# Weight splits earlier by GpSimd, the high part of x first, and spare matmuls moved in a two-layer network on one core

## The chip, the cores and the metric

The kernel runs on one core of a Trainium2 chip (trn2). The metric is the device time of one execution in microseconds (us), all of the network from its inputs in HBM to its output there. The kernel before takes 2657.98 us, the median of 3 runs (2656.43 to 2665.24).

The engines are named as the profile names them: PE (TensorE matmuls), PEld (its weight loads), DVE (VectorE), ACT (ScalarE), POOL (GpSimd), SP (SyncE, which here only issues the loads of weights).

## What is computed

Three layers on 512 tokens of width 1024, in float32, from the reference:

```python
# layer 0: h += norm(gmlp(norm(h)));  h += norm(sq_relu_mlp(norm(h)))            hidden 4096
# layer 1: k, v = norm(h) @ w_k, w_v; h += norm(band attention(norm(h), k, v)); h += norm(sq_relu_mlp(norm(h)))
def gmlp_spatial_gating(h, w_in, ln_g, ln_b, w_s, b_s, w_out):
    u, v = split(gelu(h @ w_in));  v = layer_norm(v);  return (u * (w_s masked @ v + b_s)) @ w_out
# block 2
h = h + 0.5 * swiglu(rms_norm(h), w_gate, w_up, w_down)                          # hidden 2816
z = rms_norm(h) @ w_in   # aq ak av iq ik iw | rq rk rv rg | ga gb
score = sum_heads(relu(iq . ik) * iw);  top 128 keys of each query;  y_a = softmax attention on these
y_r = group_norm(retention(rq, rk, rv)) * silu(rg)
h = h + (sigmoid(ga) * (y_a @ w_a) + sigmoid(gb) * (y_r @ w_b)) @ w_out
h = h + 0.5 * swiglu(...);  h = h + sigmoid(rms_norm(h) @ w_ple_gate) * (p @ w_ple_proj);  return rms_norm(h)
```

## The kernel before, in words

**Layout.** Activations lie feature-major: 8 tiles of 128 features by 512 tokens. The residual stream is `H`. A normed input is never divided by its root mean square before the product: `x = H * gain` goes into the product, and the result is scaled by `RI` (1 / rms, spread over all partitions) when it is taken out of PSUM.

**Three passes.** Every product runs in fp32r with both operands split into a high and a low part, as `WH*XH + WH*XL + WL*XH` (`three_passes`, L418): three matmuls of 128x128 by 128x512 for each of 8 tiles of the contraction.

**Units.** The weights are 411 units of 128x1024, in one order for all engines (`PRODUCTS`, L61): gmlp_v 0, gmlp_u 8, gmlp_out 16, ffn_a0 24, att_v 88, att_kq 96, att_out 112, ffn_a1 120, ffn_b1 184, mix_heads 252, ret_qk 263, ret_v 271, ret_gate 279, merge 287, mix_out 319, ffn_b2 327, ple 395. For each, SP loads `RAW[u % 4]` as soon as unit u-4 is split, and one engine pair splits it: POOL does both parts in the ranges of `POOL_RANGES` (high L362, low L365), elsewhere ACT makes the high part (`split_high`, L865) and DVE the low one (`split_low`, L1205), eight units (`AHEAD`) ahead of the unit whose result they take. The parts lie in slots: 0 to 3 are `WH`/`WL`, 4 to 7 (only inside the ranges of `WIDE`) are `WH2`/`WL2` or another free place (`weights_of`, L301). A unit is split only when the unit that had its slot is done (`slot_before`, L107).

**Synchronisation.** There is no scheduler: each engine's program is written out in order, and waits are on semaphores that count units done, evacuated, split. `split_low(u)` of the first unit behind a POOL range waits until POOL has split all of the range (L1209 and L1210); so does `split_high` for the high parts.

**Between two products.** The sum of squares `SS` needs all 8 result tiles: ACT squares (`square`, L875), DVE adds (`add_square`, L1217). PE turns it into a column (`stat`, L504), ACT takes the root, DVE the reciprocal (`recip`, L1237), PE spreads it (`spread`, L513). Then `post_and_pre` (L1257) forms the new `H` tile by tile and `pre_tile` (L1229) adds the square and writes `XL`, while ACT (`pre_norm`, L882) squares and then writes `XH`. The first group of the next product goes through all its units tile by tile (`together`, L436, or for token-major results `token_major_half`, L470), each tile as soon as its `XL` is there (semaphore `x_ready`); its own stat comes before the last tile (`before_last`). After a gated ffn this is `half_step` (L1362), which needs no stat of the branch.

**Attention.** The band attention runs in 32 pair steps, between which PE works on q, k and att_out tiles. In the mixing block, `mix_heads` gives the index queries and keys, each rotated by DVE and ACT (`rotate`, L1529); PE then needs the transposed `T` (L770) and `index_ready`. The sparse attention is two rounds (`attention_round`, L553, L970 and L1376) of 16 score tiles each, in 19 steps; step n has scores of n (L565), transposes of n-2 (L575), values of n-3 (L586), and `keep_busy` (L548, L551) issues matmuls that write a bank nobody reads.

## Time and profile before

| | |
|---|---|
| Runs | 2657.98 us median of 3 (2656.43 to 2665.24) |
| Profiled execution, its own time | 2656.32 us |
| its span, first to last instruction | 2654.5 us |
| PE busy | 2468.9 us (93%) in 11064 matmuls |
| DVE busy | 1363.6 us (51%) |
| ACT busy | 760.3 us (29%) |
| POOL busy | 609.3 us (23%) |
| mean granted TensorE clock | 0.968 of full |
| read from HBM | 218.23 MB, 83 GB/s over the span |

A busy share is a mean over the whole span. The 1.8 us between span and time lie around the span. Stretches are given as times from the span's start. Matmuls are pipelined: a 128x512 matmul is recorded with 0.39 us, and the next one starts 0.226 us after it (0.43 us at the halved clock).

### The profile page before, as it was taken

The numbers are of one execution on the slowest core, as the hardware profiler recorded it, in microseconds if no ns is written. First come the engines' busy times: TensorE is split into PE (matmuls) and PEld (weight loads), VectorE is DVE, ScalarE is ACT, GpSimd is POOL, SyncE is SP. The second block draws the span as 40 slices with busy tenths as digits, with TensorE's granted clock in tenths as the row PEclk, the third lists the DMA queues.
The fourth block names the chain that finished last, engine by engine and source line by source line (L and its number), as shares of the span: only waits on it lengthen the run. The fifth ranks groups of instructions, "written<-read, shape, count | busy, mean of one in ns | idle before, by whom it ended". The sixth has DMA issues, their size and how long they took to land.

```text
span 2654.5 us, 29957 instructions
## 1 busy us (share of the span) xinstructions
PE 2468.9 (93%) x11064; PEld 1972.6 (74%) x11064; DVE 1363.6 (51%) x1947; ACT 760.3 (29%) x1200; POOL 609.3 (23%) x283
## 2 busy tenths in 40 slices
PE   6778999989996999998999997979989997999997
PEld 5667888877665788887888886556578885888886
DVE  4546434463663643445554356797444353544464
ACT  2114323331442422333322233312322111322232
POOL 7650000024435000000000005462037875000000
PEclk9898999999998999999999998989999998999999
DMA  4222333322222233332433331121012332333321
GB/s 168 74 84 65 111 97 101 94 65 71 84 65 87 64 105 100 96 91 64 119 96 96 90 93 56 48 72 40 16 40 84 98 95 85 105 104 93 91 81 54
DMA packets 64824, 221.81 MB, mean 84 GB/s; under 512 B 7504, under 2 KB 9680, under 8 KB 64592
## 3 DMA queue, kind: packets, MB, share of 16 engines
q1 hardware_dynamic: 59184, 208.17, 26.5%
q10 hardware_dynamic: 5536, 12.19, 1.4%
q8 instruction: 73, 1.20, 0.2%
q14 instruction: 31, 0.25, 0.0%
HBM read 218.23 MB, written 2.10 MB: 83 GB/s over the span
## 4 chain that ended last, share of the span: by engine, by line
PE 81%; DVE 10%; POOL 4%; ACT 3%; issue 2%; ACTq 0%; POOLq 0%; DVEq 0%
PE PS L420 23%; PE PS L422 22%; PE PS L421 22%; PE PS L489 3%; POOL WH L362 2%; POOL WL L365 2%; PE PS L551 1%; DVE WL L1214 1%; PE PS L780 1%; PE PS L696 1%; PE PS L565 1%; PE PS L717 1%; PE PS L586 1%; PE PS L706 1%; DVE MK L1582 1%
## 5 line engine op out<-in xcount | busy, mean ns | idle before, releaser
L420 PE MATMUL PS<-XH,WH 128*128 128x512 f32 x1792 | 713.1, 398 | 40.3 <-DVE T L1433 12.5
L421 PE MATMUL PS<-XL,WH 128*128 128x512 f32 x1792 | 701.7, 392 | 0.0
L422 PE MATMUL PS<-XH,WL 128*128 128x512 f32 x1784 | 699.1, 392 | 0.0
L362 POOL TENSOR_TENSOR WH<-RAW,ONES 128x1024 fp32r<-128x1024 f32 (+1 forms) x136 | 266.1, 1957 | 1623.9 <-PE PS L422 1502.1
L1214 DVE TENSOR_TENSOR WL<-RAW,WH 128x1024 fp32r<-128x1024 f32 (+2 forms) x272 | 322.5, 1186 | 248.3 <-ACT WH L873 192.1
L420 PEld LDWEIGHTS PS<-XH,WH 128*128 128x128 f32 x1792 | 339.2, 189 | 130.3 <-issue 33.8
L420 PE MATMUL PS<-HH,WH 128*128 128x512 f32 x992 | 389.1, 392 | 2.5 <-DVE HL L1286 2.5
L422 PEld LDWEIGHTS PS<-XH,WL 128*128 128x128 f32 x1784 | 337.7, 189 | 71.9
L421 PEld LDWEIGHTS PS<-XL,WH 128*128 128x128 f32 x1792 | 339.8, 190 | 67.6
L422 PE MATMUL PS<-HH,WL 128*128 128x512 f32 x992 | 386.2, 389 | 0.0
L421 PE MATMUL PS<-HL,WH 128*128 128x512 f32 x992 | 386.1, 389 | 0.0
L873 ACT ACTIVATE WH<-RAW 128x1024 fp32r<-128x1024 f32 (+2 forms) x272 | 276.7, 1017 | 349.6 <-DVE M L1317 202.5
L365 POOL TENSOR_TENSOR WL<-RAW,WH 128x1024 fp32r<-128x1024 f32 (+1 forms) x132 | 322.4, 2442 | 10.4
L420 PEld LDWEIGHTS PS<-HH,WH 128*128 128x128 f32 x992 | 186.2, 188 | 50.0 <-issue 9.1
L422 PEld LDWEIGHTS PS<-HH,WL 128*128 128x128 f32 x992 | 186.2, 188 | 39.0
L421 PEld LDWEIGHTS PS<-HL,WH 128*128 128x128 f32 x992 | 186.3, 188 | 37.7
L1286 DVE TENSOR_TENSOR HL<-T,HH 128x512 fp32r<-128x512 f32 x108 | 74.8, 692 | 127.1 <-ACT HH L936 92.7
L489 PE MATMUL PS<-WH,XH 128*128 128x512 f32 x192 | 80.9, 421 | 47.2 <-DVE XL L1234 21.9
L1226 DVE TENSOR_TENSOR SS<-SS,T 128x512 f32<-128x512 f32 x91 | 82.9, 910 | 24.6 <-ACT T L879 24.6
L933 ACT ACTIVATE T<-T 128x512 f32<-128x512 f32 x64 | 40.5, 632 | 185.0 <-DVE T L1293 185.0
L1317 DVE TENSOR_TENSOR M<-PS,M 128x512 f32<-128x512 f32 x48 | 33.2, 691 | 107.2 <-PE PS L422 106.8
L879 ACT ACTIVATE T<-H 128x512 f32<-128x512 f32 x72 | 45.4, 631 | 140.3 <-DVE H L1263 47.8
(210 smaller groups left out, 2452.6 us busy)
## 6 DMA issues: line engine op xcount, KB each, us to landing
RAW<-in_weights SPq DMA_DIRECT2D x379, 512.0 KB, 3.5
RAW<-in_weights SPq DMA_DIRECT2D x16, 384.0 KB, 3.2
H<-in_xT ACTq DMA_DIRECT2D x8, 256.0 KB, 9.1
BIAS<-in_rel ACTq DMA_DIRECT2D x8, 256.0 KB, 3.6
RAW<-in_weights SPq DMA_DIRECT2D x8, 256.0 KB, 2.7
out<-R ACTq DMA_DIRECT2D x8, 256.0 KB, 2.2
BIAS<-in_rel ACTq DMA_DIRECT2D x8, 224.0 KB, 3.9
DECAY<-in_decay ACTq DMA_DIRECT2D x1, 1024.0 KB, 4.7
```

Of the source, the lines that this page charges most:

```text
L362: nc.gpsimd.tensor_tensor(high[:, 0:w], raw, ONES[:, 0:1].to_broadcast([P, w]), ALU.mult).then_inc(high_split, 1)
L365: nc.gpsimd.tensor_tensor(low[:, 0:w], raw, high[:, 0:w].bitcast(F32), ALU.subtract).then_inc(weights_split, 1)
L420: nc.tensor.matmul(PS[:, bank_, :], high[:, w], xh[:, k, :], start=(k == 0), stop=False)
L421: nc.tensor.matmul(PS[:, bank_, :], high[:, w], xl[:, k, :], start=False, stop=False)
L422: return nc.tensor.matmul(PS[:, bank_, :], low[:, w], xh[:, k, :], start=False, stop=stop)
L489: last = nc.tensor.matmul(PS[:, (first + j) % SLOTS, :], x[:, k, tok], wt[:, w], start=(k == 0 and n == 0), stop=(k == DT - 1 and n == 2))
L873: S.activation(weights_of(u)[0][:, 0:w], RAW[:, slot, 0:w], ACT.Copy).then_inc(high_split, 1)
L879: S.activation(T[:, sq.n % 2, :], src, ACT.Square).then_inc(sq_ready, 1)
L933: S.activation(T[:, 1, :], T[:, 0, :], ACT.Square).then_inc(act_self, 1)
L1214: V.tensor_tensor(low[:, 0:w], RAW[:, slot, 0:w], high[:, 0:w].bitcast(F32), ALU.subtract).then_inc(weights_split, 1)
L1226: V.tensor_tensor(SS[:], SS[:], T[:, slot, :], ALU.add).then_inc(ss_ready, 1)
L1286: V.tensor_tensor(HL[:, f, :], T[:, src, :], HH[:, f, :].bitcast(F32), ALU.subtract).then_inc(h_ready, 1)
```

## The change

- **Slots.** `WIDE` begins 4 units earlier before ffn_a0 (20 in place of 24), before ffn_a1 (116 for 120) and 8 earlier before ffn_b2 (323 for 331). Units 20 to 23 are split into `WLA`/`WL2` and wait for no unit; 116 to 119 into `WHB`/`WLB` (where `XH` and `XL` lay), from the end of unit 111 on; 323 to 326 into `WHX`/`WL2`, from the end of the merge (unit 318) on. 24 to 27 and 120 to 123 get slots 0 to 3, behind 16 to 19 and 112 to 115. Since the slots alternate by fours, the other end of each wide range shifts too: 88 to 91 now lie in slots 0 to 3, so 92 to 95 wait for them (before, for 84 to 87); 252 to 255 lie in slots 4 to 7, so 256 to 259 wait for 248 to 251 (before, for 252 to 255). POOL's last range ends at 331, and units 331 to 334 are split by ACT and DVE.
- **High part first.** ACT writes `XH` of a tile before it squares it. DVE writes `XL` (`low_part`) before it forms the next `H` and before it adds the square. In the first groups of gmlp_v, ffn_a0, att_v, ffn_a1, ffn_b1, mix_heads and ffn_b2, PE waits for `XH` alone (`xh_ready`), does both passes with it, and only then waits for `XL`.
- **Spare matmuls.** `keep_busy(24, 7)` is added before the wait ahead of L770; in the sparse attention the 2 spare matmuls of each of 18 steps are gone in both rounds, while the 10 before each round and the 14 in step 1 stay.

The core of the diff:

```diff
-POOL_RANGES = ((0, 28), (92, 124), (256, 335))
+POOL_RANGES = ((0, 28), (92, 124), (256, 331))
 AHEAD = 8
 
-WIDE = ((24, 92, 20), (120, 256, 116), (331, UNITS, 328))
+WIDE = ((20, 92, 16), (116, 256, 112), (323, UNITS, 319))
...
-            high = WHA[:, k - SLOTS, :] if 331 < u < 335 else WH2[:, k - SLOTS, :]
-            low = WLA[:, k - SLOTS, :] if 120 <= u < 124 else WL2[:, k - SLOTS, :]
+            high = WHX[k - SLOTS] if 323 <= u < 335 else WLA[:, k - SLOTS, :] if u < 24 else \
+                WHB[:, k - SLOTS, :] if 116 <= u < 120 else WH2[:, k - SLOTS, :]
+            low = WLB[:, k - SLOTS, :] if 116 <= u < 120 else WLX[k - SLOTS] if 124 <= u < 128 else WL2[:, k - SLOTS, :]
...
                     pool.wait_ge(landed[v % SLOTS], 16 * (v // SLOTS + 1) + step * 16)
-                    if v == 24:
-                        pool.wait_ge(x_ready, 2 * DT)
-                    elif v == 120:
-                        pool.wait_ge(x_done, 2 * DT * TT)
-                    elif v == 332:
+                    if v == FIRST["att_out"] + SLOTS:
+                        pool.wait_ge(units_done, FIRST["att_out"] + SLOTS)
+                    elif v == FIRST["mix_out"] + SLOTS:
                         pool.wait_ge(units_done, FIRST["mix_out"] + SLOTS)
                     elif slot_before(v) is not None:
                         pool.wait_ge(units_done, slot_before(v) + 1 + SLOTS + step * SLOTS)
...
                 for k in range(deepest):
                     if k == deepest - 1 and before_last:
                         before_last()
+                    if high:
+                        pe.wait_ge(xh_ready, high(k))
+                        w = slice(k * P, k * P + P)
+                        for s, (tiles, xh, xl, ready) in enumerate(units):
+                            if k == 0:
+                                pe.wait_ge(weights_split, split.next())
+                                pe.wait_ge(evacuated, bank.next())
+                            for n, part in enumerate(weights_of(first + s)):
+                                nc.tensor.matmul(PS[:, (first + s) % SLOTS, :], part[:, w], xh[:, k, :],
+                                                 start=(k == 0 and n == 0), stop=False)
+                        pe.wait_ge(ready.sem, ready.now(back=tiles - 1 - k))
+                        for s, (tiles, xh, xl, ready) in enumerate(units):
+                            last = nc.tensor.matmul(PS[:, (first + s) % SLOTS, :], weights_of(first + s)[0][:, w],
+                                                    xl[:, k, :], start=False, stop=(k == tiles - 1))
+                            if k == tiles - 1:
+                                last.then_inc(units_done, 1)
+                        continue
                     for s, (tiles, xh, xl, ready) in enumerate(units):
                         kk = k - (deepest - tiles)
...
                         k = 2 * q + kk
                         if k == DT - 1 and before_last:
                             before_last()
-                        if ready is not None:
-                            pe.wait_ge(ready.sem, ready.now(back=DT - 1 - k))
                         w = slice(kk * SEQ, kk * SEQ + SEQ)
-                        for j in range(TT):
-                            tok = slice(j * P, j * P + P)
-                            for n, (x, wt) in enumerate(((XH, high), (XL, high), (XH, low))):
-                                last = nc.tensor.matmul(PS[:, (first + j) % SLOTS, :], x[:, k, tok],
-                                                        wt[:, w], start=(k == 0 and n == 0),
-                                                        stop=(k == DT - 1 and n == 2))
+                        if high_now:
+                            pe.wait_ge(xh_ready, high_now(k))
+                        for passes in ((XH, high), (XH, low)), ((XL, high),):
+                            if ready is not None and passes[0][0] is XL:
+                                pe.wait_ge(ready.sem, ready.now(back=DT - 1 - k))
+                            for j in range(TT):
+                                tok = slice(j * P, j * P + P)
+                                for x, wt in passes:
+                                    last = nc.tensor.matmul(PS[:, (first + j) % SLOTS, :], x[:, k, tok], wt[:, w],
+                                                            start=(k == 0 and x is XH and wt is high),
+                                                            stop=(k == DT - 1 and x is XL))
...
                     if n < 16:
                         scores(n)
                     if not ahead:
-                        keep_busy(14 if n == 1 else 2, 2)
...
             xr.next(DT)
-            together(*[(DT, XH, XL, xr)] * 3, before_last=stat)
+            xp.n = 7 * DT
+            together(*[(DT, XH, XL, xr)] * 3, before_last=stat, high=lambda k: xp.now() + k + 1)
             spread(5)
             for s in range(3):
                 product(DT, XH, XL)
             v_ready = bank.now() + SLOTS
             product(DT, XH, XL)
+            keep_busy(24, 7)
             pe.wait_ge(evacuated, v_ready)
             for j in range(TT):
...
             def pre_norm(gs, free, ready, evacuates=None):
 
 
+                act.wait_ge(units_done, free + SLOTS)
                 for t in range(DT):
                     act.wait_ge(ready.sem, ready.next())
-                    square(H[:, t, :])
-                    if t == 0:
-                        act.wait_ge(units_done, free + SLOTS)
-                    for g, dst in gs:
+                    for n, (g, dst) in enumerate(gs):
                         S.activation(dst[:, t, :], H[:, t, :], ACT.Copy, scale=gain(g, t)).then_inc(xh_ready, 1)
+                        if n == 0:
+                            square(H[:, t, :])
                     if evacuates is not None:
                         split_high(evacuates + t + AHEAD)
...
+            def low_part(t, g, dh, dl, ready):
+
+                dve.wait_ge(xh_ready, xh.next())
+                V.scalar_tensor_tensor(dl[:, t, :], H[:, t, :], gain(g, t), dh[:, t, :].bitcast(F32),
+                                       ALU.mult, ALU.subtract).then_inc(ready, 1)
+
+            def square_and_rest(t, gs):
+
+                add_square(t == 0)
+                for g in gs[1:]:
+                    low_part(t, *g)
+
             def pre_tile(t, gs):
 
-                add_square(t == 0)
-                for g, dh, dl, ready in gs:
-                    dve.wait_ge(xh_ready, xh.next())
-                    V.scalar_tensor_tensor(dl[:, t, :], H[:, t, :], gain(g, t), dh[:, t, :].bitcast(F32),
-                                           ALU.mult, ALU.subtract).then_inc(ready, 1)
+                low_part(t, *gs[0])
+                square_and_rest(t, gs)
...
                 for t in range(DT + 1):
                     if t < DT:
                         z = T[:, 2 + t % 2, :]
-                        link(V.tensor_tensor(z, m[:, t, :], PS[:, 4, :], ALU.mult))
+                        V.tensor_tensor(z, m[:, t, :], PS[:, 4, :], ALU.mult).then_inc(dve_self, 1)
+                        me.next()
+                    if t:
+                        low_part(t - 1, *gs[0])
+                    if t < DT:
+                        dve.wait_ge(dve_self, me.now())
                         V.scalar_tensor_tensor(H[:, t, :], z, gain(g_out, t), H[:, t, :],
                                                ALU.mult, ALU.add).then_inc(residual, 1)
                     if t:
-                        pre_tile(t - 1, gs)
+                        square_and_rest(t - 1, gs)
...
                         z = T[:, 2 + t % 2, :]
                         V.tensor_tensor(z, src, M[:, t, :], ALU.add).then_inc(evacuated, 1)
+                    if t:
+                        low_part(t - 1, *gs[0])
+                    if t < DT:
                         dve.wait_ge(evacuated, done.now())
                         V.scalar_tensor_tensor(H[:, t, :], z, 0.5, H[:, t, :], ALU.mult, ALU.add)\
                          .then_inc(residual, 1)
                     if t:
-                        pre_tile(t - 1, gs)
+                        square_and_rest(t - 1, gs)
                         split_low(u + t - 1 + AHEAD)
```

**Where instructions move, 1.** POOL from unit 18 to unit 21 (one loop turn of units 4 to 19, its last two units, then the block that follows the loop), before:

```order
L361 REGISTER_ALU [waits weights_landed2]
L362 TENSOR_TENSOR WH_72<-RAW_71,ONES_107 128x1024 [waits units_done]
L365 TENSOR_TENSOR WL_73<-RAW_71,WH_72 128x1024 [waits weights_high_split]
L361 REGISTER_ALU [waits weights_landed3]
L362 TENSOR_TENSOR WH_72<-RAW_71,ONES_107 128x1024 [waits units_done]
L365 TENSOR_TENSOR WL_73<-RAW_71,WH_72 128x1024 [waits weights_high_split]
L380 REGISTER_ALU
L380 COMPARE_AND_BRANCH
L362 TENSOR_TENSOR WH2_74<-RAW_71,ONES_107 128x1024 [waits x_parts_ready,weights_landed0]
L365 TENSOR_TENSOR WL2_75<-RAW_71,WH2_74 128x1024 [waits weights_high_split]
L362 TENSOR_TENSOR WH2_74<-RAW_71,ONES_107 128x1024 [waits weights_landed1]
L365 TENSOR_TENSOR WL2_75<-RAW_71,WH2_74 128x1024 [waits weights_high_split]
```

and now, from the block that follows the loop through the first of the units behind it:

```order
L382 REGISTER_ALU
L382 COMPARE_AND_BRANCH
L364 TENSOR_TENSOR WLA_76<-RAW_71,ONES_116 128x1024 [waits weights_landed0]
L367 TENSOR_TENSOR WL2_75<-RAW_71,WLA_76 128x1024 [waits weights_high_split]
L364 TENSOR_TENSOR WLA_76<-RAW_71,ONES_116 128x1024 [waits weights_landed1]
L367 TENSOR_TENSOR WL2_75<-RAW_71,WLA_76 128x1024 [waits weights_high_split]
...
L364 TENSOR_TENSOR WLA_76<-RAW_71,ONES_116 128x1024 [waits weights_landed3]
L367 TENSOR_TENSOR WL2_75<-RAW_71,WLA_76 128x1024 [waits weights_high_split]
L364 TENSOR_TENSOR WH_72<-RAW_71,ONES_116 128x1024 [waits units_done,weights_landed0]
L367 TENSOR_TENSOR WL_73<-RAW_71,WH_72 128x1024 [waits weights_high_split]
```

Before, the block behind the loop is units 24 to 27 and begins with a wait for the end of the reads of `x` (`x_parts_ready`), behind units 20 to 23, which waited in the loop for `units_done`. Now it is units 20 to 23 and waits for no `units_done`, only for the landed weights; 24 and on stand behind it.

**Where instructions move, 2.** DVE in the norm ahead of att_v, tiles 1 and 2 (`T<-M,PS` and `H` are `post_and_pre`, `XL` and `HL` the low parts for the two products, `SS` the sum of squares), before:

```order
L1262 TENSOR_TENSOR T_92<-M_50,PS 128x512
L1263 SCALAR_TENSOR_TENSOR H_49<-T_92,GAIN_108,H_49 128x512 [waits dve_self]
L1226 TENSOR_TENSOR SS_93<-SS_93,T_92 128x512 [waits squares_ready,square_sum_ready]
L1234 SCALAR_TENSOR_TENSOR XL_54<-H_49,GAIN_108,XH_53 128x512 [waits high_ready]
L1234 SCALAR_TENSOR_TENSOR HL_57<-H_49,GAIN_108,HH_56 128x512 [waits high_ready]
```

and now:

```order
L1297 TENSOR_TENSOR T_101<-M_50,PS 128x512
L1258 SCALAR_TENSOR_TENSOR XL_54<-H_49,GAIN_117,XH_53 128x512 [waits high_ready]
L1303 SCALAR_TENSOR_TENSOR H_49<-T_101,GAIN_117,H_49 128x512 [waits dve_self]
L1252 TENSOR_TENSOR SS_102<-SS_102,T_101 128x512 [waits squares_ready,square_sum_ready]
L1258 SCALAR_TENSOR_TENSOR HL_57<-H_49,GAIN_117,HH_56 128x512 [waits high_ready]
```

`XL` of a tile now stands ahead of the next `H` and of the add of the square; the number of operations is the same.

**Where instructions move, 3.** PE in steps 2 and 3 of a round of the sparse attention (L565 and now L584 scores, L551 and now L570 spare matmuls, L575 and now L594 transposes, L586 and now L605 values), before:

```order
L565 MATMUL PS<-AK_63,T_92 128x384 [waits scores_read]
L551 MATMUL PS<-XH_53 128x512 x2
L575 MATMUL PS<-IDENT_106,PB_95 128x128 [waits probs_ready]
...
L565 MATMUL PS<-AK_63,T_92 128x512 [waits scores_read]
L551 MATMUL PS<-XH_53 128x512 x2
L575 MATMUL PS<-IDENT_106,PB_95 128x128 [waits probs_ready]
L575 MATMUL PS<-IDENT_106,PB_95 128x128
L584 REGISTER_ALU [waits probs_t_ready]
L586 MATMUL PS<-PTB_96,AVW_65 64x128 [waits hidden_parts_ready]
```

and now:

```order
L584 MATMUL PS<-AK_63,T_101 128x384 [waits scores_read]
L594 MATMUL PS<-IDENT_115,PB_104 128x128 [waits probs_ready]
...
L584 MATMUL PS<-AK_63,T_101 128x512 [waits scores_read]
L594 MATMUL PS<-IDENT_115,PB_104 128x128 [waits probs_ready]
L594 MATMUL PS<-IDENT_115,PB_104 128x128
L603 REGISTER_ALU [waits probs_t_ready]
L605 MATMUL PS<-PTB_105,AVW_65 64x128 [waits hidden_parts_ready]
```

Between scores and transposes nothing is left; all waits stay.

## Rows read from the trace of the kernel before

**Rows 1.** the page: shares of the chain of work that ended last, by engine

```profile
PE 81%; DVE 10%; POOL 4%; ACT 3%; issue 2%; ACTq 0%; POOLq 0%; DVEq 0%
```

**Rows 2.** waits of PE: engine, line <- releaser: us in total, times, longest us

```profile
PE PS L509 <- DVE SS L1226: 45.1, 5, 19.0
...
PE PS L770 <- DVE T L1547: 14.0, 1, 14.0
...
PE PS L420 <- POOL WL L365: 9.8, 4, 4.1
PE PS L420 <- DVE T L1305: 9.1, 1, 9.1
```

**Rows 3.** timeline, POOL and DVE, the gates of layer 0: start us, us, engine, line, operation [idle before]

```profile
133.64 2.35 POOL L365 TENSOR_TENSOR WL<-RAW,WH 128x1024 fp32r<-128x1024 f32 x1
...
133.80 2.73 DVE L1443 TENSOR_TENSOR T<-T,R 128x512 f32<-128x512 f32 x1
...
137.37 0.69 DVE L1443 TENSOR_TENSOR T<-T,R 128x512 f32<-128x512 f32 x1
```

**Rows 4.** timeline, PE and ACT, the end of gmlp_out and the start of ffn_a0

```profile
204.08 1.86 PE L509 MATMUL PS<-ONES,SS 128*128 128x1 f32 x8 [18.12 <-DVE SS L1226]
...
210.20 0.63 ACT L879 ACTIVATE T<-H 128x512 f32<-128x512 f32 x1 [3.96 <-DVE H L1263]
...
212.70 0.77 PE L420 MATMUL PS<-XH,WH 128*128 128x512 f32 x1 [4.11 <-DVE XL L1234]
```

**Rows 5.** timeline, DVE, the norm ahead of att_v, two tiles in a row

```profile
592.89 0.74 DVE L1234 SCALAR_TENSOR_TENSOR XL<-H,GAIN,XH 128x512 fp32r<-128x512 f32 x1
...
596.20 0.74 DVE L1234 SCALAR_TENSOR_TENSOR XL<-H,GAIN,XH 128x512 fp32r<-128x512 f32 x1
```

**Rows 6.** timeline, DVE, the last pair steps of the band attention

```profile
786.27 2.55 DVE L1513 TENSOR_SCALAR PROB<-PROB,RECX 128x512 f32<-128x512 f32 x1
```

**Rows 7.** timeline, POOL and DVE, the end of att_out

```profile
833.10 1.90 POOL L362 TENSOR_TENSOR WH<-RAW,ONES 128x1024 fp32r<-128x1024 f32 x1
...
850.36 1.22 DVE L1214 TENSOR_TENSOR WL<-RAW,WH 128x1024 fp32r<-128x1024 f32 x1 [21.44 <-POOL WLA L365]
```

**Rows 8.** timeline, DVE, the rotations of mix_heads

```profile
1622.65 0.68 DVE L1531 TENSOR_TENSOR T<-PS,RI 128x512 f32<-128x512 f32 x1
...
1630.05 0.68 DVE L1531 TENSOR_TENSOR T<-PS,RI 128x512 f32<-128x512 f32 x1
...
1652.75 0.69 DVE L1531 TENSOR_TENSOR T<-PS,RI 128x512 f32<-128x512 f32 x1
...
1657.44 0.28 DVE L1560 TENSOR_SCALAR SC<-RELU,AVW 128x128 f32<-128x128 f32 x1
```

**Rows 9.** the chain of waits in order of time (start us, us, what), sparse attention

```profile
1838.18 1.05 PE PS L565 x2
1839.24 0.66 PE PS L551 x2
...
1847.65 0.62 PE PS L565
```

**Rows 10.** groups of DVE by line, 1826 to 1910 us: xcount | busy us, mean ns | idle before

```profile
L1601 DVE TENSOR_TENSOR PB<-PS,MK 128x256 f32<-128x256 f32 (+3 forms) x31 | 15.4, 496 | 26.4 <-PE PS L565 26.3
L1389 DVE TENSOR_REDUCE NM<-PB 128x1 f32<-128x256 f32 (+3 forms) x31 | 15.3, 493 | 1.1
...
L1396 DVE TENSOR_SCALAR PB<-PB,REC 128x128 f32<-128x128 f32 (+3 forms) x32 | 12.4, 387 | 1.1
...
L1395 DVE RECIPROCAL REC<-SUM 128x1 f32<-128x1 f32 x32 | 4.9, 154 | 0.7 <-ACT PB L980 0.7
```

**Rows 11.** timeline, PE, the first product of ffn_b2

```profile
2206.81 0.80 PE L420 MATMUL PS<-XH,WH 128*128 128x512 f32 x1 [3.40 <-POOL WL L365]
```

**Rows 12.** windows: us, PE PEld DVE ACT POOL busy, PE clock, DMA share, GB/s

```profile
1640.40:1657.50 17.10, 6.85 (x17) 4.23 (x17) 12.41 (x14) 6.26 (x12) 7.09 (x3) 0.50 0.21 65
1819.50:1910.00 90.50, 89.88 (x417) 54.95 (x418) 52.60 (x144) 37.75 (x105) 0.00 (x0) 1.00 0.02 6
```

37 lines of the change are left out of this document (23 added, 14 removed).

## The prediction

> **What bounds the kernel now.** The page first: the chain of work that ended last is PE for 81% of the span, DVE for 10% and POOL for 4% [rows 1]. So only what PE waits for can be won. The table of PE's waits names it next [rows 2]: 45.1 us in five waits for the last sum of squares, the longest 19.0; 14.0 us ahead of the transposes at L770; 9.8 us for low weight parts that POOL makes, all at the start of ffn_b2; 9.1 us for DVE one product later. The timelines then tell what is late behind each name. Last come the windows, for the clock [rows 12]: in the stretch after the 14 us wait PE is granted 0.50 of full speed (1.2 GHz) for 17.1 us, in the sparse attention 1.00. A wait of PE therefore costs twice: itself, and work that runs at half pace behind it.
>
> The second thing to price is how POOL and DVE get in each other's way, since the change moves 20 unit splits of POOL forward, beside DVE's work. In the gates of layer 0 a DVE multiply of two SBUF operands takes 2.73 us when POOL's low part (2.35 us) has just begun, and 0.69 us three microseconds later [rows 3]: 2.04 us lost. A unit has two POOL operations, so up to 4.1 us of DVE per unit. In the rotations one head takes 7.40 us beside POOL (1622.65 to 1630.05) and 4.69 us without (1652.75 to 1657.44) [rows 8], 2.7 us lost in 7.4, or 1.8 us per 4.9 us of splitting. The gates are the nearer row where DVE works back to back; a DVE operation may come in the middle of POOL's, so I take 3.4 us per unit there. By the Trainium skill (GPSIMD Engine Reference, Specifications) the SBUF interfaces of GpSimd are shared with VectorE, with contention for DVE instructions that have two SBUF inputs. It speaks against splitting earlier. By the rule the trace agrees, 2.73 against 0.69 us. An account without that rule would price all moved splits at nothing: rival A.
>
> **The terms.** All against the profiled execution's own 2656.3 us. Parts with one answer go together.
>
> 1. *Start, gmlp_v.* `XH` ahead of the square lets PE begin its two high passes earlier, but the tiles come in by DMA, and only the order of ACT's two operations changes. POOL's operations fall elsewhere among DVE's. +1.5 (-3 to +4).
>
> 2. *gmlp_out (units 20 to 23 early).* The wait for the sum at its end is 18.12 us [rows 4], since DVE may split unit 28 on only when POOL has finished 24 to 27, and then squares. POOL is through one block of four earlier. Without contention the wait shrinks to about 2.6 (the last tile's evacuation, square and add, 0.6 to 0.7 each as such operations take [rows 3, 4], and handoffs): -15.6. But 20 to 23 are now split while the gates run: 8 two-input operations of DVE lose 2.04 each, 16.3. PE starts the product late and is paced by `XL`. Some lies in slack; I take 11.6: **-4.0** (bounds -15.6 and +0.7).
>
> 3. *High first at ffn_a0, ffn_a1, ffn_b1.* PE waits 4.11 us for the first `XL` [rows 4]. `XH` came behind the square of 0.63 us and was followed by DVE's next `T`, `H`, the copy and `XL`. `XH` can now be made where the square was, from 210.20 on, and stands at 210.9; the high passes start then instead of at 212.70 and cover DVE's low part: -1.7 each, **-5.1** (-7 to -2). The square is later by one ACT operation, 0.7, which the 8 tiles' DVE cadence hides.
>
> 4. *att_v.* DVE sets the pace, five operations and 3.31 us per tile (592.89 to 596.20) [rows 5]. Units 92 to 95 used to wait for 84 to 87; now for 88 to 91, so 92 to 94 are split beside these very operations, four in five of which have two SBUF inputs. 3 units x 3.4 = 10.2, less 3.5 of slack that PE leaves and high first, plus 1.2 of slow clock: **+7.6** (-1 to +12).
>
> 5. *Pair steps (116 to 119 early).* They are now split back to back from the end of unit 111. A DVE scale of one pair step already takes 2.55 us beside POOL [rows 6], and there its steps are near PE's pace. Four units x 3.4 = 13.6 bounds it, half and more is slack: **+4.0** (0 to +8).
>
> 6. *att_out.* This is the clearest one. DVE's low part at 850.36 stood 21.44 us, released by POOL's `WLA`, since POOL began unit 120 only at 833.10 [rows 7]: four units of 4.8 us behind the reads of the attention output. Now 116 to 119 are done before, 120 to 123 take the place of 116 to 119, and DVE comes free 17 us earlier, about 833. Late next is the last square itself: the 19.0 us wait [rows 2] becomes 2.6: **-16.4** (-19 to -10).
>
> 7. *mix_heads.* 256 to 259 start four units of PE earlier (4 x 24 x 0.226 = 22 us), since they wait for 248 to 251 and not for 252 to 255. They slow the half step ahead (+2), then leave two or three of the rotations free of POOL, 2.7 us each. L770 starts some 3.6 us earlier. `keep_busy(24, 7)` takes 24 x 0.23 = 5.4 us at full clock (about 10 at half), which ends inside a wait of 10 or more; the gain in clock is about 1.5. Sum **-5.0** (-9 to 0). If the wait were shorter than the spare matmuls, they would cost what reaches over.
>
> 8. *Sparse attention.* Two spare matmuls are 0.66 us in each step [rows 9], 18 steps, two rounds: 23.8 at most. In four steps PE spends 9.47 (1838.18 to 1847.65) [rows 9], without the spare ones 6.83. What comes next is the ring of two steps: scores of n-1, DVE's add and maximum, the scaling of n-2, its transposes, values of n-3, scores of n+1. By means: PE 9.47/4 less 0.66 = 1.71 of scores, transposes and values; DVE 0.496 + 0.493 + 0.154 + 0.387 = 1.53 [rows 10]; handoffs, five of about 0.1, an estimate. That is 3.7 to 3.8 for two steps, 7.6 for four, and as the long steps of PE and DVE do not coincide, near 8.2. (9.47 - 8.2) x 4.5 = 5.9 a round: **-11.8** (0 to -23.8, where the ring does or does not bind throughout).
>
> 9. *ffn_b2 (323 to 326 early, 331 to 334 by ACT and DVE).* POOL's last unit is 330, and it begins as soon as the merge ends. The 9.8 us for low parts go [rows 2]. The group at 2206.81 [rows 11] then starts when DVE gives `XL` tiles, still 2.5 us behind where the waits summed would put it; the 9.1 us for `T` [rows 2], which DVE made late as it had waited for POOL, go; 2.2 of slow clock behind these waits goes. -9.8 - 9.1 - 2.2 + 2.5 = **-18.6** (-23 to -14).
>
> Sum: +1.5 - 4.0 - 5.1 + 7.6 + 4.0 - 16.4 - 5.0 - 11.8 - 18.6 = -47.8, so 2608.5, told as **2609**. The median of the runs is 1.7 above the profiled execution, less than the sum is sure of.
>
> **The rivals.**
>
> *A, contention is light, or the ring is slack.* For it: POOL is busy 23% of the span only, and a DVE operation that comes between POOL's is not held. Against: rows 3 show 2.04 us at once. Then term 2 is -15.6, term 4 -1, term 5 nothing: -24 more, **2584**. The full 23.8 of term 8 alone would give 2597.
>
> *B, contention is heavy.* Each of the 20 moved units costs PE its whole 3.4 us: 68 instead of the 23 counted in terms 2, 4 and 5: 45 more, **2654**, no change. For it: DVE is the pace in att_v. Against: most moved splits lie beside products of PE that have DVE idle (it is busy 51%).
>
> *C, the clock falls in the sparse attention.* It ends slower. Its steps stay at 1.00 now [rows 12] with spare matmuls of full width in each; without them PE has short matmuls and transposes, 6.83 of 8.2 us. At 1.2 GHz its own work in four steps is 13.7 us, over the ring, and each round 13.7 x 4.5 + 3.9 of head = 65.5 against 46.2 now: +38.6 for two in place of -11.8, and some 5 for the retention head behind at half clock: **2664**, slower than before by 0.3%; each us that att_v or the gates lose above my terms goes on top. Below a granted clock of 0.72 the steps' own work (6.83/0.72 = 9.5) gives back term 8; to end slower than before it needs the lower clock through both rounds. Against it: PE stays over 80% busy. The Trainium skill (TensorE: Matmul & The Clock Gate, Part 4: PE-mode transpose) says that full clock does not engage for transposes, which do not count as busy the same way. No run here shows this by itself so far.
>
> *D, the change does less than it says:* the ring holds steps at 9.4 us already, term 8 is nothing, **2620**.
>
> **The numbers.** Forecast 0.60 (D is in its range), A 0.17, B 0.14, C 0.09. A measurement of this kernel can tell about 0.3%, 8 us, from no change. The bounds of the unknown terms, added as independent, give some 20 about the forecast; the range takes in A to 2587 and most of B, to 2648, and leaves out C and the low end of A. Faster by over 0.3% is the forecast, A, and B's better part, 0.60 + 0.17 + 0.09 = 0.86; within 0.3%, the rest of B and half of C, 0.09; slower 0.05.
>
> **What would show it.** Right: the wait for the sum ahead of ffn_a1 is 2 to 4 us; no wait of PE for POOL's low part ahead of ffn_b2, whose first tile starts near 6 us after where it did; rows at 0.77 and 2.7 us side by side on DVE in the gates; four sparse steps in 8.2 us at clock 1.00. Wrong: att_out's wait still over 10 us (then DVE is held by something else); sparse steps at 9.4 or 6.9 us per four; a PE clock under 1.00 there; a wait for POOL in att_v ahead of unit 96.

## The result, and the profile after

The changed kernel takes 2638.28 us (median of 4 runs, 2633.09 to 2638.75) where the kernel before, run beside it, takes 2660.94 (2656.43 to 2665.24). The ratio is 0.9911, 95% interval 0.9887 to 0.9934: faster by 0.9%, 22.7 us between the medians, about half of the 47.8 that were forecast. The profiled execution has a span of 2636.9 us (before 2654.5) and a mean clock of 0.961 (before 0.968). It is the slowest of its four runs, and the one before is the fastest, so the stages below differ by 17.6 us in all.

Stage by stage in the two profiled executions, each stage from the first instruction named to the next one's:

| Stage | before, us | after, us | difference | forecast |
|---|---|---|---|---|
| start to the wait ahead of the gates | 95.6 | 97.1 | +1.5 | +1.5 |
| to the first tile of ffn_a0 | 117.1 | 109.2 | -7.9 | -5.7 |
| ffn_a0, to the sum ahead of att_v | 357.2 | 356.9 | -0.3 | 0 |
| att_v, to the first tile of its second product | 64.2 | 75.0 | +10.8 | +7.6 |
| pair steps and att_out, to the sum | 226.5 | 212.6 | -14.0 | -12.4 |
| ffn_a1 and ffn_b1, to the sum in mix_heads | 750.2 | 748.1 | -2.1 | -3.4 |
| mix_heads, to the transposes of the index inputs | 39.8 | 33.8 | -6.0 | -5.0 |
| to the first retention tile (index scores, sparse attention) | 264.7 | 283.4 | **+18.7** | **-11.8** |
| to the first tile of ffn_b2, and from there to the end | 739.1 | 720.8 | -18.3 | -18.6 |

All rows but one came within 3.2 us of the forecast. The chain of work that ended last, by engine, in the changed kernel (before [rows 1]):

```profile
PE 80%; DVE 12%; ACT 3%; issue 2%; POOL 2%; ACTq 0%; POOLq 0%; DVEq 0%
```

POOL went from 4% of the chain to 2%, DVE from 10 to 12. The waits of PE in the changed kernel (engine, line <- releaser: us in total, times, longest):

```profile
PE PS L528 <- DVE SS L1252: 19.6, 7, 4.6
...
PE PS L422 <- DVE T L1476: 12.5, 1, 12.5
...
PE PS L453 <- ACT XH L915: 7.4, 3, 2.5
PE PS L508 <- POOL WL L367: 7.2, 2, 3.6
...
PE PS L594 <- DVE PB L1439: 4.2, 7, 0.9
...
PE PS L453 <- DVE H L1707: 3.5, 2, 2.3
...
PE PS L795 <- DVE T L1590: 2.4, 1, 2.4
```

Against [rows 2]: the sums fell from 45.1 us to 19.6, the longest from 19.0 to 4.6; the index inputs' 14.0 are 2.4; POOL's 9.8 at ffn_b2 (L420, now L453) are gone, and 3.5 for `H` stand there instead; the 9.1 are gone too. The 12.5 us ahead of the gates are as they were. Nothing in this table tells of a loss of 19 us in the sparse attention: it isn't a wait. The windows show it (us, then busy time of PE, PEld, DVE, ACT, POOL, then PE clock, DMA share, GB/s), the whole of the two rounds in the changed kernel:

```profile
1801.00:1821.90 20.90, 18.91 (x84) 11.50 (x83) 17.18 (x45) 8.90 (x24) 1.20 (x1) 1.00 0.09 26
1821.90:1852.60 30.70, 29.84 (x89) 16.96 (x90) 12.58 (x35) 9.69 (x30) 0.00 (x0) 0.50 0.00 1
1852.60:1866.30 13.70, 12.15 (x55) 7.70 (x53) 6.31 (x19) 6.18 (x15) 0.00 (x0) 1.00 0.00 1
1866.30:1910.70 44.40, 43.47 (x129) 24.85 (x130) 17.85 (x48) 13.04 (x39) 0.00 (x0) 0.50 0.00 0
```

PE is granted 1.00 for the first 20.9 us, then 0.50 (1.2 GHz) for 30.7, 1.00 for 13.7 and 0.50 for 44.4. Before, both rounds had 1.00 [rows 12]. The timeline of PE, the scores of steps four apart, at either clock:

```profile
1812.33 0.49 PE L584 MATMUL PS<-AK,T 64*128 64x128 f32 x2
...
1820.44 0.48 PE L584 MATMUL PS<-AK,T 64*128 64x128 f32 x2
...
1827.27 1.65 PE L584 MATMUL PS<-AK,T 64*128 64x384 f32 x2
...
1840.80 1.01 PE L584 MATMUL PS<-AK,T 64*128 64x384 f32 x1
```

Four steps take 8.11 us at full clock (1812.33 to 1820.44; 8.2 was forecast, 9.47 before [rows 9]) and 13.53 at half (1827.27 to 1840.80). The 13.7 us at 1.00 in the middle are not plain steps: they lie around the end of the first round and hold the 10 and 14 full-width spare matmuls of the second round's head (from 1853.83 and 1857.81 on).

### The profile page after: what moved, and what is told of

It is laid out like the page before. It is cut to its first block, busy times and chain, and to the rows that moved or that the text cites. A ratio compares the mean times of both kernels' runs of the same rounds, so it can differ in the third digit from the quotient of the medians.

```text
span 2636.9 us, 29784 instructions
## 1 busy us (share of the span) xinstructions
PE 2494.5 (95%) x11016; PEld 1986.7 (75%) x11016; DVE 1397.0 (53%) x1951; ACT 764.5 (29%) x1204; POOL 594.9 (23%) x275
## 4 chain that ended last, share of the span: by engine, by line
PE 80%; DVE 12%; ACT 3%; issue 2%; POOL 2%; ACTq 0%; POOLq 0%; DVEq 0%
PE PS L422 22%; PE PS L424 21%; PE PS L423 21%; PE PS L453 2%; PE PS L508 2%; PE PS L457 1%; PE PS L605 1%; DVE MK L1625 1%; PE PS L584 1%; DVE SS L1252 1%; DVE TOP L1624 1%; POOL WL L367 1%; PE PS L805 1%; PE PS L717 1%; PE PS L738 1%
## 5 line engine op out<-in xcount | busy, mean ns | idle before, releaser
L422 PE MATMUL PS<-XH,WH 128*128 128x512 f32 x1600 | 634.7, 397 | 18.1 <-DVE T L1476 12.5
L424 PE MATMUL PS<-XH,WL 128*128 128x512 f32 x1632 | 638.1, 391 | 0.0
L423 PE MATMUL PS<-XL,WH 128*128 128x512 f32 x1600 | 625.2, 391 | 0.0
L364 POOL TENSOR_TENSOR WH<-RAW,ONES 128x1024 fp32r<-128x1024 f32 (+1 forms) x123 | 239.9, 1950 | 1589.8 <-DVE WL L1240 735.9
L422 PEld LDWEIGHTS PS<-XH,WH 128*128 128x128 f32 x1600 | 302.0, 189 | 98.3 <-issue 20.9
L424 PEld LDWEIGHTS PS<-XH,WL 128*128 128x128 f32 x1632 | 307.8, 189 | 65.2
L423 PEld LDWEIGHTS PS<-XL,WH 128*128 128x128 f32 x1600 | 302.4, 189 | 60.2
L367 POOL TENSOR_TENSOR WL<-RAW,WH 128x1024 fp32r<-128x1024 f32 (+1 forms) x123 | 300.5, 2443 | 9.6
L1252 DVE TENSOR_TENSOR SS<-SS,T 128x512 f32<-128x512 f32 x91 | 91.7, 1008 | 24.6 <-ACT T L905 24.6
L508 PE MATMUL PS<-WL,XH 128*128 128x512 f32 x192 | 81.6, 425 | 0.0
```

Of the source, the lines that this page charges most:

```text
L364: nc.gpsimd.tensor_tensor(high[:, 0:w], raw, ONES[:, 0:1].to_broadcast([P, w]), ALU.mult).then_inc(high_split, 1)
L367: nc.gpsimd.tensor_tensor(low[:, 0:w], raw, high[:, 0:w].bitcast(F32), ALU.subtract).then_inc(weights_split, 1)
L422: nc.tensor.matmul(PS[:, bank_, :], high[:, w], xh[:, k, :], start=(k == 0), stop=False)
L423: nc.tensor.matmul(PS[:, bank_, :], high[:, w], xl[:, k, :], start=False, stop=False)
L424: return nc.tensor.matmul(PS[:, bank_, :], low[:, w], xh[:, k, :], start=False, stop=stop)
L508: last = nc.tensor.matmul(PS[:, (first + j) % SLOTS, :], x[:, k, tok], wt[:, w], start=(k == 0 and x is XH and wt is high), stop=(k == DT ...
```

## Experiments

Theory: all terms hold but the one of the sparse attention, whose spare matmuls were what kept the clock. Rival: contention of POOL and DVE ate the gain. Each run is compared with the kernel before on the same chip, so across experiments the ratios are safer to compare than the times. Lines in the rows are those of the version that ran; where its edit adds lines, they lie a few further down than in the changed kernel. Stages and rows come from one profiled execution each.

### 1. The spare matmuls back

```diff
-                        keep_busy(14 if n == 1 else 0, 2)
+                        keep_busy(14 if n == 1 else 2, 2)
```

> The changed kernel with the 2 spare matmuls back in each step of the sparse attention; all else as changed. Theory (clock): the sparse attention alone lost the rest, because PE falls to 1.2 GHz in it. Then the granted clock of both rounds is 1.00 again, four steps take 9.47 us as before the change, the stretch is some 18 us shorter than in the changed kernel, and the time is 2618 to 2622 us, ratio to before 0.984 to 0.986. Rival (contention): the early splits of POOL lost it, the sparse stretch moves by under 5 us and the time stays at 2633 to 2640.

2619.45 us (2614.43 to 2626.42), ratio 0.9856 (0.9833 to 0.9878). The two rounds in the windows of this version:

```profile
1798.00:1842.50 44.50, 44.33 (x209) 27.25 (x210) 26.74 (x73) 17.17 (x51) 0.00 (x0) 1.00 0.01 4
1842.50:1887.00 44.50, 43.80 (x207) 26.57 (x205) 23.88 (x66) 18.18 (x52) 0.00 (x0) 1.00 0.00 0
```

Clock 1.00 throughout. The stretch from the transposes of the index inputs to the first retention tile is 262.8 us, within 2 us of what it was before the change, and the median is 18.8 us below that of the changed kernel (by the two ratios, 0.9911 and 0.9856, it is 14.6; the intervals don't touch). The theory holds, the rival doesn't.

### 2. Only this part, in the kernel before

```diff
-                        keep_busy(14 if n == 1 else 2, 2)
+                        keep_busy(14 if n == 1 else 0, 2)
```

> The kernel before with one part of the change: no spare matmuls in the steps of the sparse attention. Theory (clock): this part by itself costs; the clock falls to 0.50 within the first round, four steps go from 9.47 to 13.5 us there, and the time is before + 15 to 20, ratio 1.006 to 1.008. Rival (the fall needs another part of the change, such as the earlier start or the 24 spare matmuls ahead): clock 1.00, four steps in 8.1 us, ratio 0.995 to 0.996. Third case: as the clock falls at a time that lies differently to the steps, the loss may be anywhere from 5 to 39 us.

2678.01 us (2664.50 to 2679.96), ratio 1.0067 (1.0050 to 1.0084): slower, 19 us by the medians. The windows of the rounds:

```profile
1819.00:1850.10 31.10, 27.81 (x128) 16.31 (x126) 24.25 (x67) 14.37 (x41) 0.80 (x1) 1.00 0.06 18
1850.10:1867.20 17.10, 16.30 (x54) 10.29 (x54) 5.44 (x15) 4.29 (x13) 0.00 (x0) 0.50 0.00 1
1867.20:1887.60 20.40, 18.34 (x82) 10.86 (x81) 12.07 (x35) 10.08 (x27) 0.00 (x0) 1.00 0.00 0
1887.60:1918.30 30.70, 29.84 (x91) 17.29 (x91) 11.99 (x32) 9.02 (x27) 0.00 (x0) 0.50 0.00 0
```

The same fall, without any other part of the change. Counted from the first spare matmul ahead of the rounds (1815.17, in the changed kernel 1797.58) it begins 35 us in, not 24, and 47.8 us of the rounds are at 0.50 in place of 75.1; this profiled execution (2664.5) is the mildest of its five. When the fall begins varies; it came in both executions that were profiled, and the other four times are longer still.

### 3. One spare matmul per step

```diff
-                        keep_busy(14 if n == 1 else 0, 2)
+                        keep_busy(14 if n == 1 else 1, 2)
```

> The changed kernel with 1 spare matmul in each step in place of 0. PE's own work in four steps is then 6.83 + 4 x 0.33/1.45 = about 7.7 to 8.15 us, the ring of DVE and PE gives about 8.2 to 8.6. Theory (clock, held by what PE does in the steps): if one spare matmul holds the clock, four steps take about 8.6 us, the time is 8 us below the version with two, 2610 to 2614, ratio 0.981 to 0.983. If it does not hold it, the steps take about 15 us at half clock, and the time is that of the changed kernel or more, 2636 to 2655. Rival (contention): within 5 us of the changed kernel's 2638 either way.

2616.21 us (2613.31 to 2622.03), ratio 0.9840 (0.9818 to 0.9861). Both rounds at clock 1.00:

```profile
1797.00:1842.00 45.00, 43.76 (x200) 26.48 (x198) 31.66 (x82) 18.59 (x52) 2.98 (x2) 1.00 0.05 15
1842.00:1887.00 45.00, 43.15 (x203) 25.85 (x202) 24.15 (x66) 19.18 (x53) 0.00 (x0) 1.00 0.00 0
```

One holds the clock as two do. Four steps take 9.0 us, not the expected 8.6: PE waits once in four steps, behind the 512-wide scores, and runs back to back in the other three, so a spare matmul in those costs its whole time, 0.3 us (9.01 us against 8.11 for three of them). From the start of ret_v to the first retention tile it is 4.5 us less than with two (146.5 against 151.0).

### 4. The spare matmuls only where PE waits

```diff
-                        keep_busy(14 if n == 1 else 0, 2)
+                        keep_busy(14 if n == 1 else 4 if n % 4 == 0 else 0, 2)
```

> The changed kernel with 4 spare matmuls in every fourth step (the one whose transposes wait for DVE's scaling behind the 512-wide scores) and none in the others: as many in four steps as with one per step, but all where PE waits, 1.28 us in each four steps. Theory (the clock needs enough matmul work per stretch, no matter in which step): clock 1.00 in both rounds, four steps in 8.1 to 8.3 us in place of 9.0, so 7 to 8 us below the version with one spare per step: 2608 to 2610. Rival (the three steps without any pull the clock down): clock 0.50 in part of the rounds as in the changed kernel, four steps up to 14 to 15 us, 2632 to 2640.

2611.04 us (2609.69 to 2618.37), ratio 0.9826 (0.9808 to 0.9844).

```profile
1796.00:1840.00 44.00, 43.28 (x208) 27.11 (x207) 31.37 (x82) 18.71 (x52) 2.80 (x2) 1.00 0.05 16
1840.00:1884.00 44.00, 42.70 (x199) 26.21 (x198) 24.06 (x66) 19.29 (x53) 0.00 (x0) 0.96 0.00 0
```

The clock holds but for a moment (0.96 in the second round), and from the start of ret_v to the first retention tile it is 1.7 us less than with one per step. Less than expected: four steps take 8.4 us, and step 0 got 4 spare matmuls where it had 1, which costs 0.7 in each round.

### 5. Units 20 to 23 as before

```diff
-WIDE = ((20, 92, 16), (116, 256, 112), (323, UNITS, 319))
+WIDE = ((24, 92, 20), (116, 256, 112), (323, UNITS, 319))
```

with two spare matmuls per step, and POOL's wait for the reads of `x` ahead of unit 24 as before the change.

> The changed kernel with 2 spare matmuls per step and with units 20 to 27 and so the slots up to unit 91 as before the change (20 to 23 wait in slots 0 to 3, 24 to 27 wide; 92 to 95 wait for 84 to 87 again). Theory (terms by stage hold): gmlp_out and its sum's wait lose the gain of 6 us, att_v gains 12.8 us back as POOL no longer splits 92 to 95 beside the norm's DVE operations (3.3 us a tile as before instead of longer). So 6 us faster than the version with the two spare matmuls alone: 2612 to 2616. Rival (POOL and DVE do not hurt each other in att_v, the loss there is from the new order of low part and square): att_v stays 12 us longer, and the time is 2624 to 2628.

2619.57 us (2618.74 to 2626.54), ratio 0.9846 (0.9830 to 0.9863): as experiment 1, no gain. By stages both parts are there: ffn_a0's first tile comes 7.2 us later behind the gates' wait (the sum's wait is 18.1 again, as in [rows 4]), and att_v takes 68.5 us in place of the 74.6 of experiment 1. It was expected to fall back to 64. DVE's tiles take 3.2 us there; the rest is 13.6 us at 0.50 behind the sum where before the change it was 3.4. The profiled execution is the longest of the four and loses 5.2 us more ahead of the gates, where the edit changes nothing. Inconclusive for the time, since the terms cancel; experiment 6 tells it.

### 6. Units 16 to 19 early in their place

```diff
-WIDE = ((20, 92, 16), (116, 256, 112), (323, UNITS, 319))
+WIDE = ((16, 92, 12), (116, 256, 112), (323, UNITS, 319))
...
-            high = WHX[k - SLOTS] if 323 <= u < 335 else WLA[:, k - SLOTS, :] if u < 24 else \
+            high = WHX[k - SLOTS] if 323 <= u < 335 else WLA[:, k - SLOTS, :] if u < 20 else \
```

with POOL's waits ahead of unit 24, and one spare matmul per step. Then the alternation by fours comes out as before the change: 92 to 95 lie in slots 0 to 3 and wait for 84 to 87.

> The changed kernel with 1 spare matmul per step, and in place of units 20 to 23 now units 16 to 19 lie in the early place and wait for no unit; 20 to 23 wait in slots 0 to 3 for 12 to 15, 24 to 27 lie wide and wait for 20 only, so that 92 to 95 wait for 84 to 87 as before the change. Theory (contention in att_v costs about 6 us there, the early split in gmlp_out brings 6): both are had, the stat ahead of ffn_a0 stays at a wait of 2.2 us, att_v's tiles on DVE take 3.2 us, and the time is 5 to 8 us below the version with one spare matmul (2616): 2608 to 2611, ratio 0.981 to 0.983. Rival (the gates' contention moves to an earlier product and the gain of gmlp_out goes with it): 2614 to 2620.

2607.41 us (2601.01 to 2608.16), ratio 0.9806 (0.9790 to 0.9823), 8.8 us below the version with one spare. att_v takes 64.1 us; in the version with one spare it was 77.7. (Some of that is chance: six profiled executions with the same att_v code, those of the changed kernel and of experiments 1, 3, 4, 8 and 12, took 74.6 to 77.7.) What POOL does to DVE there is seen in the changed kernel, timelines of POOL and DVE:

```profile
583.01 2.35 POOL L364 TENSOR_TENSOR WH<-RAW,ONES 128x1024 fp32r<-128x1024 f32 x1 [1.88 <-PE PS L508]
585.44 2.69 POOL L367 TENSOR_TENSOR WL<-RAW,WH 128x1024 fp32r<-128x1024 f32 x1
594.17 1.97 POOL L364 TENSOR_TENSOR WH<-RAW,ONES 128x1024 fp32r<-128x1024 f32 x1 [6.04 <-PE PS L508]
596.23 2.68 POOL L367 TENSOR_TENSOR WL<-RAW,WH 128x1024 fp32r<-128x1024 f32 x1
```

```profile
583.52 0.68 DVE L1297 TENSOR_TENSOR T<-M,PS 128x512 f32<-128x512 f32 x1
584.12 1.78 DVE L1258 SCALAR_TENSOR_TENSOR XL<-H,GAIN,XH 128x512 fp32r<-128x512 f32 x1
585.83 2.85 DVE L1303 SCALAR_TENSOR_TENSOR H<-T,GAIN,H 128x512 f32<-128x512 f32 x1
...
594.32 2.38 DVE L1303 SCALAR_TENSOR_TENSOR H<-T,GAIN,H 128x512 f32<-128x512 f32 x1
596.62 2.83 DVE L1252 TENSOR_TENSOR SS<-SS,T 128x512 f32<-128x512 f32 x1
```

and of PE, at the end of the same tiles:

```profile
601.43 0.80 PE L528 MATMUL PS<-ONES,SS 128*128 128x1 f32 x3 [4.62 <-DVE SS L1252]
```

Two DVE operations that start 0.39 us after POOL's low part take 2.85 and 2.83 us where they otherwise take 0.74 and 0.68, and those beside POOL's high parts 1.78 and 2.38 where they otherwise take 0.74. All four end 0.54 to 0.56 us after the POOL operation they started beside, and so do the two beside the unit before (576.49 and 579.40, 2.38 and 2.28 us long). `T`, which reads one of its inputs from PSUM, took 0.68 in the middle of one (583.52). For the three units that is 3.2, 3.2 and 3.8 us of DVE, 10.1 together, and PE waits 4.62 us for the sum. In experiment 6 every tile takes 3.19 us (585.06 to 588.25 for two low parts in a row):

```profile
585.06 0.75 DVE L1261 SCALAR_TENSOR_TENSOR XL<-H,GAIN,XH 128x512 fp32r<-128x512 f32 x1
...
588.25 0.75 DVE L1261 SCALAR_TENSOR_TENSOR XL<-H,GAIN,XH 128x512 fp32r<-128x512 f32 x1
```

The rival had a point too. Earlier splits cost elsewhere: the wait ahead of the gates is 19.7 us instead of 12.5, and the sum ahead of ffn_a0 waits 6.84, not 2.2:

```profile
199.47 1.87 PE L531 MATMUL PS<-ONES,SS 128*128 128x1 f32 x8 [6.84 <-DVE SS L1255]
```

### 7. att_v low first

```diff
-            products_token_major(xr, stat, lambda k: xp.now() + 2 * k + 1)
+            products_token_major(xr, stat)
```

PE then waits for the low part ahead of all three passes there. One spare matmul per step.

> The version with 1 spare per step, but PE in the first half of att_v waits for the low part of each tile before all three passes, as before the change; DVE's order stays new. Theory (high first there lets PE catch up with DVE, which sets the pace, so that it stands at the sum and its clock falls): no or a short wait at the stat, att_v from its first stat to the second half's start 3 to 5 us shorter, 2611 to 2613. Rival (contention with POOL alone makes att_v longer): same as the version with one spare, 2615 to 2618.

2614.22 us (2611.54 to 2616.96), ratio 0.9834 (0.9818 to 0.9851), against 2616.21 with high first; the intervals overlap. att_v takes 77.8 us against 77.7. The forecast 3 to 5 us don't show: high first there costs nothing that these runs can tell, though one profile of each, where the same code varies by 3 us, wouldn't show less.

### 8. Without the 24 ahead of the transposes

```diff
-            keep_busy(24, 7)
```

with one spare matmul per step.

> The version with 1 spare per step, without the 24 spare matmuls ahead of the transposes of the index inputs. Theory (they lie in a wait and only keep the clock): the wait ahead of the transposes is 8 to 10 us long, they start at the same moment, and some 1.5 to 3 us are lost at half clock behind it: 2617 to 2620. Rival (the clock gate needs them not, or they delay the transposes): 0 to 2 us faster, 2614 to 2616.

The ten runs gave 2614.76 once, 2649.78 to 2661.29 nine times, median 2658.37. Neither expectation has it. The windows, from 1631.1 us on, the index scores:

```profile
1631.10:1733.50 102.40, 97.21 (x170) 45.15 (x171) 39.68 (x55) 26.44 (x52) 19.06 (x9) 0.50 0.07 21
```

The clock fell 5.2 us ahead of the transposes (1636.29), inside a wait of 7.81, and stayed: PE is busy for 97.2 of 102.4 us, all of it at 0.50. This is work of three full-width matmuls to one narrow score. In the changed kernel the same work is at 1.00 but for 6.8 us.

### 9. The 24 alone, in the kernel before

```diff
             product(DT, XH, XL)
+            keep_busy(24, 7)
             pe.wait_ge(evacuated, v_ready)
```

> The kernel before with one part of the change alone: the 24 spare matmuls ahead of the transposes of the index inputs. Theory (they shorten the idle time from 14 to about 8 us and so the stretch at 0.50 behind it from 17 to 7 to 14 us): 1.5 to 5 us faster than before, ratio 0.998 to 0.9995; the transposes start at the same moment. Rival (as in the version without them, the wait of 8 us that they leave may be followed by 100 us at 0.50): 2680 to 2700, ratio 1.01 or more, or very different single runs.

2658.89 us (2656.39 to 2697.21, 10 runs), ratio 0.9996 (0.9986 to 1.0006, without the run of 2697.21). The half-clock stretch goes from 17.1 us to 6.8 in the profile, but most of the 17.1 lies inside the wait: PE works 6.85 us of it, and 3.5 of the 6.8. The time doesn't move beyond its uncertainty. One run of ten took 2697.21, and one of seven of the kernel before in another comparison 2698.91; neither was profiled.

### 10. Low first in all first groups

Experiment 6 with `high=` and `high_now` left out of all calls, so that PE waits for the low part ahead of the three passes everywhere.

> The version with units 16 to 19 early and 1 spare per step, but PE waits for the low part of each tile before all three passes in all first groups, as before the change; the orders of ACT and DVE stay new. Theory (high first starts each of four groups 1.7 us earlier, but at half clock, so 1.0 to 1.3 us each are left): 4 to 6 us slower than with high first, 2611 to 2614, the waits ahead of these groups 3.1 to 3.4 us in place of 2.45. Rival (it gives nothing since DVE sets the pace within the groups): 2606 to 2609.

2650.05 us (2646.14 to 2651.90), ratio 0.9963 (0.9949 to 0.9977). Not the 4 to 6 us slower that were expected, but 43, and the stages say why: the index scores again.

```profile
1629.60:1725.20 95.60, 95.60 (x165) 44.09 (x166) 34.99 (x49) 23.91 (x48) 17.05 (x8) 0.50 0.06 17
```

PE is busy for all of 95.6 us, at 0.50, although the 24 spare matmuls are there and the wait behind them is the 2.39 us that it is in experiment 6.

### 11. The same with 34

```diff
-            keep_busy(24, 7)
+            keep_busy(34, 7)
```

> The version with low first everywhere, which lost 96 us of clock in the index scores although it had 24 spare matmuls ahead (2650 us), now with 34. Theory (an idle time of 2.4 us ahead is what started the fall): clock 1.00 or at most 7 to 10 us at 0.50 in the index scores, and the time 2606 to 2613. Rival (the fall has nothing to do with the idle time ahead): 2646 to 2652 again.

2606.93 us (2603.45 to 2609.31), ratio 0.9798 (0.9780 to 0.9815), 43 below experiment 10. The wait ahead is filled (0.12 us are left), and the index scores and the products behind them run at full clock:

```profile
1622.00:1715.00 93.00, 92.58 (x342) 58.18 (x341) 71.52 (x99) 32.17 (x63) 46.48 (x21) 1.00 0.19 56
```

From one sum to the next in the profiles, high first (experiment 6 against this one) is worth 2.0 us at ffn_a0, 0.9 in att_v's first half, 0.5 at ffn_a1 and 0.3 at ffn_b1, 3.7 together. The times don't show it: 2607.41 with high first and 24, 2606.93 here.

### 12. And with 12

```diff
-            keep_busy(24, 7)
+            keep_busy(12, 7)
```

with one spare matmul per step, high first.

> The version with 1 spare matmul per step (2616 us) with 12 in place of 24 ahead of the transposes: 2.7 us of work, so some 5 us idle. Theory (idle time ahead decides, and without any 9 of 10 runs took 2650 to 2661): most runs at 2650 to 2660, some 100 us at 0.50 in the index scores. Rival (it is a matter of the moment at which the stretch begins, not of the idle time): runs spread over 2615 and 2655, or all near 2616.

Four runs: 2614.34, 2618.14, 2654.40, 2660.31. Neither expectation alone: with 5.1 us idle ahead two runs are some 40 us longer and two aren't. The profile is that of 2618.14, with 10.2 us at 0.50. That the longer two lost their time in the index scores is argued from experiment 8; their mean clock, 0.958 and 0.959 against 0.974 and 0.975, says only that it was lost to the clock.

### 13. 48 spare matmuls ahead of the retention's values

```diff
             products(XH, XL)
-            products_token_major()
             pe.wait_ge(relu_done, 32)
+            keep_busy(48, 7)
+            products_token_major()
```

in experiment 6.

> The version with units 16 to 19 early and 1 spare per step, with 48 spare matmuls (10.9 us) in the 13.9 us wait ahead of the values of the retention, after a wait for the last index score's reader. Theory (what the 24 do ahead of the transposes can be had here too): the product starts at the same moment and the 13.7 us at clock 0.50 behind the wait go or become 3 to 7: 3 to 6 us faster, 2601 to 2605. Rival (the added wait or the spare matmuls delay the product, or PE is not granted full clock for them): 0 to 5 us slower.

2605.18 us (2602.32 to 2612.02), ratio 0.9802 (0.9784 to 0.9821), 2607.41 without: no difference that can be told. The stretch at 0.50 went from 13.7 us to 3.4, but most of the 13.7 lay inside the wait: PE worked 4.6 us of it, and 3.1 of the 3.4. The product started 1.3 us later and the retention no earlier. A half clock costs only what PE works under it.

### 14. Both improvements, and the wait filled

Experiment 6 with 4 spare matmuls in steps 4, 8, 12 and 16; then the same with 34 in place of 24.

> Both improvements at once: units 16 to 19 early in place of 20 to 23, and in the sparse attention 4 spare matmuls in steps 4, 8, 12 and 16 alone. Theory (both gains are real and in different stretches): att_v as in the version with units 16 to 19 early (64 us from its first sum to its second half), four steps of the sparse attention in 8.1 to 8.5 us at clock 1.00, 2602 to 2606 us, ratio 0.979 to 0.981. Rival (the clock of the sparse stretch is near its edge and falls when the stretch starts elsewhere in time): part of the rounds at 0.50 and 2612 to 2630.

> The fastest version so far (units 16 to 19 early, 4 spare matmuls in every fourth step of the sparse attention) with 34 in place of 24 spare matmuls ahead of the index inputs' transposes, 7.7 us of a wait of 7.8. Theory (the stretch behind falls only where PE has stood idle ahead of it): the wait left is 0 to 0.2 us, no stretch at 0.50 behind it, the time the same within 2 us, 2598 to 2602 (that version had none there either). Rival (the spare matmuls reach over the wait): up to 2 us slower.

2600.93 us (2597.52 to 2605.95), ratio 0.9784 (0.9767 to 0.9802), and 2599.64 us (2598.61 to 2613.37), ratio 0.9790 (0.9757 to 0.9824). These beat both kernels: 2.1% under the one before, 38 us under the changed one. Between the two there is no difference beyond the intervals, and that of 0.9784 overlaps experiment 6's too.

## Why the prediction was wrong, point by point

- **Term 8, the sparse attention, failed.** It said -11.8 us with a clock of 1.00, and the stretch gave +18.7: 30 us, all of the miss, since the other terms sum to -36.0 and measured -36.3. The two prices in it were right (8.11 us for four steps against 8.2, and 13.53 at half clock against the 13.7 of rival C; a slip of 0.2 a round, 1.27 x 4.5 being 5.7 and not 5.9, changes nothing). What was mis-judged was which of the two holds. The step that failed is that the clock stays at 1.00 without the spare matmuls, on the ground that "PE stays over 80% busy". PE was busy for 18.91 of 20.9 us at the end of which the clock fell. Rival C happened for 75 of the 110 us of the two rounds, and was given a chance of 0.09. The experiments 1 and 2 show the cause: with the spare matmuls back the clock stays and 14.6 to 18.8 us come back; their removal alone costs the kernel before 19.
- **The range was luck.** 2638 lies inside the 2587 to 2648 of the prediction, but the upper end was there for rival B, contention, and rival C, which happened in part, was left out of it.
- **The rule named beside rival C.** The Trainium skill (TensorE: Matmul & The Clock Gate, Part 4: PE-mode transpose) says that full clock doesn't engage for transposes. The sparse steps would agree with it (0.50), and with one spare matmul each they had 1.00, transposes and all (experiment 3). But the index scores have no transposes in them, and stayed at 0.50 for 102 and 96 us too; it can't be the whole of it.
- **Term 2, gmlp_out:** -5.7 with high first, measured -7.9. The wait for the sum went from 18.12 to 2.24 us. Contention is there, operations of the gates taking 1.66 and 2.83 us in the changed kernel; the multiply takes 0.69 without POOL [rows 3], and so did the low part (137.97 in the trace of before):

```profile
146.53 2.83 DVE L1489 TENSOR_TENSOR XL<-T,XH 128x512 fp32r<-128x512 f32 x1
...
149.99 1.66 DVE L1486 TENSOR_TENSOR T<-T,R 128x512 f32<-128x512 f32 x1
```

- **Term 3, high first:** -5.1 forecast for three groups. The waits went from 4.11 us [rows 4] to 2.45, as forecast, but PE starts at half clock and gives part back: 2.8 by the sums in experiments 6 and 11 (2.0, 0.5, 0.3).
- **Term 4, att_v:** +7.6 forecast (its own addends give 7.9), +10.8 measured; the mechanism is that of experiment 6, and its 10.2 us for three units were right (10.1). What is left of the difference is mostly clock: PE worked 16.5 us of this stage at 0.50, and 9.5 before, 3.5 us more where the term had 1.2.
- **Terms 5 and 6:** -12.4 forecast, -14.0 measured. DVE's low part of the first unit behind POOL's range waited for POOL for 4.26 us instead of 21.44 [rows 7], and the sum's wait went to 2.24 as said:

```profile
840.19 1.23 DVE L1240 TENSOR_TENSOR WLX<-RAW,WH 128x1024 fp32r<-128x1024 f32 x1 [4.26 <-POOL WL L367]
...
850.06 0.69 DVE L1252 TENSOR_TENSOR SS<-SS,T 128x512 f32<-128x512 f32 x1 [0.76 <-ACT T L905]
```

```profile
850.80 0.27 PE L528 MATMUL PS<-ONES,SS 128*128 128x1 f32 x1 [2.24 <-DVE SS L1252]
```

  It stood until 840.2, not 833; that cost nothing, for the last square ends the stage.
- **Term 7, the index inputs:** -5.0 forecast, -6.0 measured. The transposes start at 1632.65, behind the 24 spare matmuls (the row shows the last ten) and a wait of 2.39:

```profile
1627.84 2.43 PE L570 MATMUL PS<-XH 128*128 128x512 f32 x10
1632.65 0.66 PE L795 MATMUL PS<-IDENT,T 128*128 128x128 f32 x4 [2.39 <-DVE T L1590]
```

  But the 1.5 us of clock in the term rest on a misreading. The 17.1 us at half clock [rows 12] don't follow the 14 us wait: they begin at 1640.4, and the transposes before the change come only at 1650.65. PE works 6.85 us of them. In the changed kernel it works 6.70 us at 0.50, as before:

```profile
1650.65 1.11 PE L770 MATMUL PS<-IDENT,T 128*128 128x128 f32 x4 [13.96 <-DVE T L1547]
```

```profile
1634.20:1641.00 6.80, 6.70 (x15) 3.99 (x15) 3.71 (x8) 3.23 (x7) 0.00 (x0) 0.50 0.01 2
```

  What the 24 matmuls do was not in the term at all: without them nine runs of ten are some 40 us longer (experiment 8).
- **Term 9, ffn_b2:** -18.6 forecast, -18.3 measured. No wait for POOL's low parts is left there; two for `H`, 3.5 us, took its place.
- **Rival A** (no contention) is out by att_v. **Rival B** (each moved unit costs PE 3.4 us) is out by the stages, **rival D** (the steps keep their 9.4 us) by the 8.11. The rule that GpSimd and VectorE share their SBUF interfaces (the Trainium skill, GPSIMD Engine Reference, Specifications) agrees with the changed kernel's 2.85 us against 0.74, shown in experiment 6.

What stays open: why the index scores fall in some versions and runs and not in others. It isn't the idle time ahead alone. A wait of 14.0 us in the kernel before was followed by 6.85 us of work at half clock, 7.81 in experiment 8 by 97, and 2.39 by 95.6 in experiment 10, by 6.7 in the changed kernel and by none in experiments 1 and 6. Filled waits never showed it: none of the eight runs of experiments 11 and 14's second version is over 2614. Terms 5, 6 and 9, the largest gains, were only read from the two profiles; no run changes them alone. Nor was it tried which of a step's matmuls hold the clock in the sparse attention, their width or their number.

## What to carry to other kernels

Spare matmuls on a busy PE look like pure cost in the chain of waits; price their removal at both clocks, and don't dismiss the lower one because PE stays busy: here it was 90% busy when the clock fell. Put them where PE waits, not in every step, and try filling a wait ahead of such a stretch wholly: behind one of 2 to 8 us here, the index scores lost some 40 us in some versions and runs. Before you price a half-clock stretch, take off the part that lies inside the wait. When an edit changes how buffers alternate, look at the far end of the range: four units moved at one end put others beside DVE's work 70 units later, and moving the other four cured it.

## What the runs showed of the hardware

- With PE busy for 95.6 of 95.6 us the granted clock stayed at 0.50 (index scores of experiment 10), and the same program with ten more spare matmuls ahead had 1.00 for 93 us, over the same work and more (experiment 11).
- In the sparse attention 75.1 of 109.7 us were at 0.50 with PE 97% and 98% busy in them (changed kernel). With one 128x512 spare matmul per step both rounds had 1.00 (experiment 3). Without any, the clock came back in the changed kernel at 1852.6, 1.2 us ahead of the next spare matmuls, and fell again 5 us behind the last of them.
- One program can have two times 40 us apart on one chip: 2614.34 and 2654.40 (experiment 12), and the kernel before 2657.78 and 2698.91.
- A DVE operation with two inputs in SBUF that starts beside a POOL one ended 0.54 to 0.56 us after POOL's in six of six cases in att_v (changed kernel), so it took 1.78 to 2.85 us for 0.74 or 0.68. One such operation is lost per POOL operation; the next takes 0.7 us unless POOL has begun another.
